# One decoder trunk: the recurrence's square root by a correction step, decay masks as a bound, and the compression with token rows stationary

## The reference, cut to what matters

```python
# NSA: compressed keys and values, 15 blocks of 32 tokens
def compress(t, pe, w):
    ch = t.reshape(B, S // CMP_STRIDE, CMP_STRIDE, d)
    blk = jnp.concatenate([ch[:, :-1], ch[:, 1:]], axis=2)
    return ((blk + pe).reshape(B, nc, CMP_LEN * d) @ w).astype(F32)

# RG-LRU
log_a = -LRU_C * r * jax.nn.softplus(-lam.astype(F32))
a = jnp.exp(log_a)
b = jnp.sqrt(jnp.maximum(-jnp.expm1(2.0 * log_a), 0.0)) * (i_g * xb)
_, h = lax.associative_scan(comb, (a, b), axis=1)      # h_t = a_t h_(t-1) + b_t

# SSD, for each chunk of 128 tokens: Lm is lower triangular
Lm = jnp.exp(segsum(a))
scores = jnp.einsum('bclhn,bcshn->bhcls', Cc, Bc) * Lm
y_diag = jnp.einsum('bhcls,bcshp->bclhp', scores, x)
```

## Time and profile before

| what | us |
|---|---|
| median of 3 runs | 1559.27 (1558.99 to 1560.87) |
| the profiled execution, device time | 1556.36 |
| its span, from first to last instruction | 1554.8 |
| PE busy | 1516.8 (98%) |
| DVE busy | 1249.4 (80%) |
| ACT busy | 1006.7 (65%) |
| loop of the mixers, layer 0 and layer 1 | about 82 to 139 and 481 to 536 |

### The profile page before, as it was taken

One profiled execution on the slowest core, in us unless ns is written; L12 is line 12 of the kernel. 1 busy time (PEld: TensorE's weight loads), 2 busy tenths in 40 slices (PEclk: granted clock), 3 DMA queues, 4 the chain that ended last, 5 costly groups with the idle time before them and its releaser, 6 DMA issues.

```text
span 1554.8 us, 20132 instructions
## 1 busy us (share of the span) xinstructions
PE 1516.8 (98%) x7391; PEld 1272.0 (82%) x7391; DVE 1249.4 (80%) x1296; ACT 1006.7 (65%) x926; POOL 81.5 (5%) x109
## 2 busy tenths in 40 slices
PE   8999999999999899999999999999999999999996
PEld 6987888888798788878888888888888888888885
DVE  6888654455567879998988898899889889889986
ACT  6465534433446647777777777777777777778764
POOL 3101000000000010000000000000000000000000
PEclk9997999999999799999999999999999999999998
DMA  9702655556440049999999999999999999999991
GB/s 316 235 1 59 227 190 189 189 183 195 159 167 1 1 176 341 395 390 353 393 393 348 394 396 347 394 395 346 394 395 344 395 396 343 396 397 346 394 396 59
DMA packets 189820, 444.23 MB, mean 286 GB/s; under 512 B 9697, under 2 KB 15982, under 8 KB 189758
## 3 DMA queue, kind: packets, MB, share of 16 engines
q1 hardware_dynamic: 185206, 427.81, 75.0%
q0 software_dynamic: 4528, 15.58, 3.8%
q10 hardware_dynamic: 24, 0.01, 0.0%
HBM read 435.51 MB, written 7.86 MB: 285 GB/s over the span
## 4 chain that ended last, share of the span: by engine, by line
PE 94%; DVE 3%; ACT 1%; issue 1%; DMA 0%; SPq 0%; POOL 0%; POOLq 0%; DVEq 0%; ACTq 0%
PE bank L439 27%; PE bank L440 27%; PE bank L438 26%; PE bank L569 2%; PE bank L495 2%; PE bank L698 1%; PE bank L572 1%; PE bank L718 1%; PE bank L675 1%; PE bank L727 0%; DVE hT L2051 0%; PE bank L690 0%; PE bank L934 0%; DMA work<-in_nsa_cmp_pe_dram 0%; PE bank L600 0%
## 5 line engine op out<-in xcount | busy, mean ns | idle before, releaser
L1729 DVE TENSOR_TENSOR w_lo<-ring,w_hi 128x2048 fp32r<-128x2048 f32 x372 | 846.5, 2290 | 176.8 <-ACT w_hi L1305 175.8
L1305 ACT ACTIVATE w_hi<-ring 128x2048 fp32r<-128x2048 f32 x372 | 711.8, 1916 | 223.9 <-PE bank L438 223.9
L439 PE MATMUL bank<-w_hi,xT_hi 128*128 128x512 f32 x896 | 353.8, 395 | 0.5 <-DVE xT_lo L2314 0.5
L440 PE MATMUL bank<-w_hi,xT_lo 128*128 128x512 f32 x896 | 349.7, 390 | 0.0
L438 PE MATMUL bank<-w_lo,xT_hi 128*128 128x512 f32 x896 | 240.0, 390 | 0.0
L439 PE MATMUL bank<-w_hi,hidT_hi 128*128 128x512 f32 x560 | 221.0, 395 | 2.8 <-DVE hidT_lo L1736 2.8
L440 PE MATMUL bank<-w_hi,hidT_lo 128*128 128x512 f32 x560 | 218.5, 390 | 0.0
L438 PEld LDWEIGHTS bank<-w_lo,xT_hi 128*128 128x128 f32 x896 | 168.3, 188 | 35.4
L439 PEld LDWEIGHTS bank<-w_hi,xT_hi 128*128 128x128 f32 x896 | 168.3, 188 | 34.5 <-DVE xT_lo L2314 0.7
L440 PEld LDWEIGHTS bank<-w_hi,xT_lo 128*128 128x128 f32 x896 | 168.6, 188 | 33.5
L439 PE MATMUL bank<-w_hi,hT_hi 128*128 128x512 f32 (+2 forms) x384 | 146.8, 385 | 2.7 <-DVE hT_lo L1685 2.7
(11 more groups left out here) (370 smaller groups left out, 1359.0 us busy)
## 6 DMA issues: line engine op xcount, KB each, us to landing
ring<-in_moe_w_gate_dram SPq DMA_DIRECT2D x112, 1024.0 KB, 9.5
ring<-in_moe_w_up_dram SPq DMA_DIRECT2D x112, 1024.0 KB, 9.5
ring<-in_moe_w_down_dram SPq DMA_DIRECT2D x112, 1024.0 KB, 9.2
ring<-in_ffn_w_gate_dram SPq DMA_DIRECT2D x14, 1024.0 KB, 5.1
ring<-in_ffn_w_up_dram SPq DMA_DIRECT2D x14, 1024.0 KB, 5.1
ring<-in_ffn_w_down_dram SPq DMA_DIRECT2D x14, 1024.0 KB, 4.8
ring<-in_w_in_dram SPq DMA_DIRECT2D x12, 1024.0 KB, 6.6
ring<-in_w_out_dram SPq DMA_DIRECT2D x8, 1024.0 KB, 7.2
```

Of the source, the lines that this page charges most:

```text
L439: pe.matmul(o, x_hi, w, start=start, stop=False)
L440: return pe.matmul(o, x_lo, w, start=False, stop=False)
L1305: act.activation(w_hi[:, (base + at) % SPLIT, :], ring[:, i, :], ACT.Copy).then_inc(hi_ready, 1)
L1729: dve.tensor_tensor(w_lo[:, v, :], ring[:, (base + at) % RING, :], w_hi[:, v, :].bitcast(F32), ALU.subtract).then_inc(lo_ready, 1)
```

## The change

- The recurrence. Before, with t = tanh(log_a/2), DVE computed 1/(1 - t) with its reciprocal. Now ACT computes exp(log_a) as well, DVE forms (1 + exp)/2 from it, which is 1/(1 - t) but for rounding, and betters it with one correction step of two instructions. The pieces stand at other steps: the correction and the first `lb` in step 3, the rest of `lb` and `lt2` in step 6, between the first products of `yd` and its sums, with `lt1` and `lgate` ahead of those sums as well.
- The decays. A new constant `dbound` (made by POOL) is 0 where a decay counts and -1e30 where it doesn't. The decay tiles are bounded by it with the minimum that took 0 before, so their exponentials come out as zeros there, and the two mask multiplications go.
- `ssd_sums`, and what DVE does with it, moves from step 3 to step 4, on PE between `scores(4)` and `products(2)`, on DVE behind `score_rows(4)`. Its three fillers go.
- The compression. Before, the weights (128 columns, keys and values together) were stationary and 30 columns of tokens moved, 16 matmuls, with three fillers between. Now the 15 token rows are stationary and 64 columns of weights move, 32 matmuls without fillers. The result lies by rows, so the values need no turning, and the keys do (`turn_keys`). DVE copies it ahead of the convolution of step 2, no longer behind it.
- At the start of layer 0 DVE makes the low part of the first weights between the second and the third group of `hT_lo`, no longer after all four and after the copies of the parameters.

```diff
@@ mixer buffers, constants (POOL)
+        dbound = sb("dbound", [P, 2 * P])
...
+            link(pool.memset(dbound[:, :], 0.0))
...
+            link(pool.affine_select(out=dbound[:, 0:P], in_=dbound[:, 0:P], compare_op=ALU.is_ge, fill=NEG, base=0,
+                                    pattern=[[1, P]], channel_multiplier=-1))
@@ PE
-                def compress(b, idle):
+                def compress(b):
 
                     pe.wait_ge(cin_ready, l + 1)
-                    for j in range(CLEN // 2):
-                        mm = pe.matmul(b[:, 0:2 * NC], w_cmp[:, j, :], cin[:, j, :, :].rearrange("p c n -> p (c n)"),
-                                       start=(j == 0), stop=(j == CLEN // 2 - 1))
-                        if j in (3, 7, 11):
-                            keep_busy(idle, 1)
+                    for c in range(2):
+                        for j in range(CLEN // 2):
+                            mm = pe.matmul(b[0:NC, c * HD:(c + 1) * HD], cin[:, j, c, :], w_cmp[:, j, c * HD:(c + 1) * HD],
+                                           start=(j == 0), stop=(j == CLEN // 2 - 1))
                     give(mm, 0)
 
-                def turn_values():
+                def turn_keys():
 
                     pe.wait_ge(cmp_ready, 2 * l + 1)
                     b = bank(0)
-                    give(pe.transpose(b[0:NC, 0:HD], kcv[HD:P, 1, :], ident[HD:P, HD:P]), 0)
+                    give(pe.transpose(b[0:HD, 0:NC], ckv[0:NC, 0:HD], ident[0:NC, 0:NC]), 0)
...
                 def ssd_sums():
 
                     b = bank(0)
-                    keep_busy(b, 3)
                     pe.wait_ge(ssd_act, 3 * l + 2)
...
                     if n < len(AJ):
                         scores(n)
+                    if n == 4:
+                        ssd_sums()
                     if n >= 2:
                         products(n - 2)
...
                     if n == 3:
-                        turn_values()
-                        ssd_sums()
+                        turn_keys()
@@ ACT, step 1
-                        act.activation(lt2[:, :, :], la[:, :, :], ACT.Tanh, scale=0.5).then_inc(lru_act, 1)
+                        act.activation(lt2[:, :, :], la[:, :, :], ACT.Tanh, scale=0.5)
+                        act.activation(ld[:, :, :], la[:, :, :], ACT.Exp).then_inc(lru_act, 1)
@@ DVE, start of layer 0
-                split_turned(2 * l)
+                if l > 0:
+                    split_turned(2 * l)
                 if l == 0:
+                    split_turned(0, (0, 1))
+                    split(p)
+                    split_turned(0, (2, 3))
...
-                    split(p)
                 split(p + 1)
@@ DVE, the loop
+                    if n == 4:
...
+                        take_bank(dve.tensor_copy(xtok[:, :, :], b[:, :].rearrange("p (t c) -> p t c", t=TB)))
...
+                                link(dve.scalar_tensor_tensor(out=dec0[:, h, :], in0=b[:, i * S:(i + 1) * S],
+                                                              scalar=nacs[:, 0, h:h + 1], in1=dbound[:, :],
+                                                              op0=ALU.add, op1=ALU.min))
+                                ins = dve.scalar_tensor_tensor(out=dec1[:, h, :], in0=b[:, i * S + P:(i + 1) * S],
+                                                               scalar=nacs[:, 1, h:h + 1], in1=dbound[:, 0:P],
+                                                               op0=ALU.add, op1=ALU.min)
...
                     if n == 2:
+                        b = filled()
+                        take_bank(dve.tensor_copy(ckv[0:NC, :], b[0:NC, 0:2 * HD]))
+                        signal(dve.tensor_copy(flag[:, 0:1], ones[:, 0:1]), "cmp", cmp_ready)
                         signal(conv(xbc, xraw, "scw", "scb", 6, 4, 6), "ssd_conv", ssd_conv)
-                        b = filled()
-                        take_bank(dve.tensor_copy(kcv[:, :, :], b[:, 0:2 * NC].rearrange("p (c n) -> p c n", c=2)))
-                        signal(dve.tensor_copy(flag[:, 0:1], ones[:, 0:1]), "cmp", cmp_ready)
...
-                    if n == 4:
+                    if n == 3:
 
                         dve.wait_ge(lru_act, 5 * l + 2)
-                        link(dve.tensor_scalar(ld[:, :, :], lt2[:, :, :], -1.0, 1.0, ALU.mult, ALU.add))
-                        link(dve.reciprocal(ld[:, :, :], ld[:, :, :]))
-                    if n == 5:
+                        link(dve.tensor_scalar(ld[:, :, :], ld[:, :, :], 0.5, 0.5, ALU.mult, ALU.add))
+                        link(dve.scalar_tensor_tensor(out=lb[:, :, :], in0=lt2[:, :, :], scalar=-1.0, in1=ld[:, :, :],
+                                                      op0=ALU.add, op1=ALU.mult))
+                        link(dve.scalar_tensor_tensor(out=ld[:, :, :], in0=lb[:, :, :], scalar=2.0, in1=ld[:, :, :],
+                                                      op0=ALU.add, op1=ALU.mult))
                         link(dve.scalar_tensor_tensor(out=lb[:, :, :], in0=lt2[:, :, :], scalar=-4.0, in1=ld[:, :, :],
                                                       op0=ALU.mult, op1=ALU.mult))
-                        signal(dve.scalar_tensor_tensor(out=lb[:, :, :], in0=lb[:, :, :], scalar=0.0,
...
                     if n == 5:
 
                         dve.wait_ge(ssd_act, 3 * l + 3)
-                        tri = upper[:, :].unsqueeze(1).broadcast_to([P, SSD_H, P])
-                        link(dve.tensor_tensor(dec0[:, :, 0:P], dec0[:, :, 0:P], tri, ALU.mult))
-                        link(dve.tensor_tensor(dec1[:, :, :], dec1[:, :, :], tri, ALU.mult))
...
                     if n == 6:
...
+                        signal(dve.scalar_tensor_tensor(out=lb[:, :, :], in0=lb[:, :, :], scalar=0.0,
+                                                        in1=ld[:, :, :], op0=ALU.max, op1=ALU.mult),
+                               "lru_vec", lru_vec)
+                        link(dve.scalar_tensor_tensor(out=lt2[:, :, :], in0=lt2[:, :, :], scalar=1.0, in1=ld[:, :, :],
+                                                      op0=ALU.add, op1=ALU.mult))
```

More of the change, by code:

```diff
@@ L529, in _ @@
                 p = BASE_MIX[l]
[L530 removed]
+                (qtok, kcat, vtok, xb, xbc, qT, kT, nqT, kswT, kcT, ckv, nacs, cin, xtok, xdt, dec1, kvT2,
                  dec0) = mix_bufs[l]
@@ L1674, in lam_start, with split_turned @@
                        "half_b", half_b_ready)
-            def split_turned(norm):
+            def split_turned(norm, groups=range(4)):
                 l, which = divmod(norm, 2)
                 c0 = PR["ffn" if which else "mix"]
-                for g in range(4):
+                for g in groups:
                     b = filled()
@@ L2021, in _ @@
                         b = filled()
[L2022 removed]
+                        take_bank(dve.tensor_copy(kcT[0:HD, :], b[0:HD, 0:NC]))
                         signal(dve.tensor_copy(flag[:, 0:1], ones[:, 0:1]), "cmp", cmp_ready)
[L2025 to L2030 removed]
@@ L2092, in _ @@
                                                       op0=ALU.add, op1=ALU.mult))
+                        for tb in range(TB):
+                            b = filled()
+                            take_bank(dve.tensor_tensor(yd[:, tb, :], yd[:, tb, :], b[:, 0:GW], ALU.add))
+                        signal(dve.tensor_tensor(yd[:, :, :], yd[:, :, :], zs[:, :, :], ALU.mult), "ssd_vec", ssd_vec)
                     if n == 7:
```

64 lines of the change are left out of this document (24 added, 40 removed).

## The result

| | before | changed |
|---|---|---|
| median | 1559.51 (1558.99 to 1560.87, 4 runs) | 1545.53 (1542.24 to 1546.42, 4 runs) |
| the profiled execution | 1556.36 | 1542.24 |
| ratio | | 0.991, 95% interval 0.9897 to 0.9922 |

The forecast was 1554.4, 4.9 us less, with 1547.5 as the lower end of its range.

A forecast was written before the change was run, and what follows sets the result against it. DVE was taken to bound both mixer loops: -10.7 there, +6.0 for the low clock, -0.2 at the start, -4.9 in all. From 1556.36 that gives 1551.5 profiled; the median, 2.9 above, 1554.4; range 1547.5 to 1562.

The forecast's parts named there:

- The stretches that bound the kernel: Both mixer loops, from DVE's copy of the compressed values to the end of lgate: 34.05 and 32.52 us, DVE the chain.
- DVE's work: Per layer in the stretch: reciprocal out -3.38, correction in +1.44, masks out -1.45, decays reading a second tensor +0.2.
- The two waits for `ssd_sums`: DVE's waits in each layer vanish, as PE runs the sums during DVE's four instructions and score_rows(4): -1.73.
- The new wait of 0.3: DVE at score_rows(4), ready at 102.7, waits for ACT's turned_probs(2), ending at 103.0: +0.3 per layer.
- The compression: Ahead of DVE's copy in step 2: 64 records at 0.06 us, done at 92.15, no loss.
- Rival 2: Compression bound by its 64 records at 0.118 each: DVE waits 3.25 us per layer in step 2, 1560.9; chance 0.18.
- The clock behind PE's gap: PE idles 2 us inside ssd_sums and the clock falls to 1.2 GHz behind it: +6.0 in all; forecast's chance 0.52.
- What the low clock costs: 6.8 us at half speed cost PE 3.4, less 0.4 to spare: DVE waits 3.0 us in each layer.
- The layer 0 wait of 1.53 in step 7: DVE's wait for PE at the low clock; taken to vanish if PE is at the high clock there.
- The tail: After lgate, to the output projection: same chain in both versions, clock taken as low as before, length unchanged within 1 us.
- The start: First low weight part ready before PE wants it: gain 0.2, the middle of 0 to 0.46.
- Rival 1: The clock doesn't fall behind PE's gap, or the gap is covered, so no 6.0 loss: 1548.4; chance 0.12.

The follow-up runs named there:

- e2: Changed kernel with the 3.38 us reciprocal back in place of the correction step, still in step 3: 1550.81 us.
- e9: e8 with the two mask multiplications put back ahead of the products of the decays: 1544.23 us.
- e3: Changed kernel with ssd_sums and DVE's part of it back in step 3, ahead of the correction, without its three fillers: 1554.45 us.
- e6: e3 with the correction moved to step 4, so sums in step 3 and correction in step 4: 1547.56 us.
- e5: Changed kernel with the two mask multiplications put back ahead of the products of the decays: 1543.50 us.
- e7: Kernel before with the move alone: ssd_sums in step 4 without its three fillers, reciprocal in step 3: 1556.51 us.
- e8: Changed kernel with ten filler matmuls per layer in PE's waits of steps 6 to 8: 1541.39 us.
- e16: Changed kernel with the correction alone moved to step 4, so sums and correction both in step 4: 1554.13 us.
- e14: e7 with the ten tail fillers of e8: 1558.80 us.
- e4: Changed kernel with three more DVE instructions of 128x512 per layer ahead of score_rows(4), to lengthen PE's gap: 1549.58 us.
- e10: e8 with e4's three extra DVE instructions per layer ahead of score_rows(4): 1547.22 us.
- e13: Kernel before with the ten tail fillers of e8 and three more ahead of products(3): 1566.48 us.
- e1: The changed kernel again, nothing edited: 1546.03 us.
- The four corners: Sums and correction each in step 3 or 4 of the changed kernel: e1 1546.0, e3 1554.5, e6 1547.6, e16 1554.1 us.

## Why the prediction was wrong

- **The stretches that bound the kernel** were the right ones: 11.2 of the 14 us come from the two mixer loops.
- **DVE's work**: -3.38 + 1.44 - 1.45 + 0.2 = -3.2 forecast per layer, -3.3 measured. The decays with `dbound` took 484 and 351 ns, as before, so 0.2 was too much. e2 gave 4.8 for the reciprocal (3.9 forecast), e9 2.8 for the masks (2.9), part of it a low stretch of the clock.
- **The two waits for `ssd_sums`** went, as forecast, but not for the reason given. With the sums back in step 3 (e3, e6) DVE doesn't wait for them either. So it was not the move that took 1.73 us per layer away, but the three fillers that went or the earlier compression; no run parts the two. The new wait of 0.3 didn't come: DVE left the correction at 102.37 and went on at 102.40, for ACT had turned the probabilities by 102.3.
- **The compression** was right. The row answers rows 6 and 9:

```profile
87.81 3.75 PE L729 MATMUL bank<-w_cmp,work 128*15 128x64 f32 x64
```

  3.67 us to the next row, over 64 records, are 0.057 each, beside the 0.06 taken. DVE's copy stood right behind `score_rows(2)` without a wait. Rival 2 is out. The eight short loads of rows 9 all lay in the low stretch from 124.5 us on, not half of them; at the high clock the new loads show 96 ns.
- **The clock behind PE's gap is the step that failed**, 6.0 of the 8.9 us. The gap was forecast well (2 us, 1.66 measured). The fault was to take the fall of rows 6 and 8 for one that any gap of at least 1.38 us brings. In the changed kernel the clock stayed at 2.4 GHz behind the gap in both layers of both profiles. The traces side by side; a fall counts if it comes within the wait or at most 1.4 us behind its end:

| PE's wait | length, us | loops | the clock |
|---|---|---|---|
| inside `ssd_sums` (changed twice, e5, e7, e8, e9, e16, layer 1 of e14) | 1.60 to 1.85 | 15 | falls in 1 (e14) |
| the same place (e2, e4, e10) | 3.53 to 3.84 | 6 | falls in 5 |
| ahead of `products(3)` (before twice, e6) | 1.38 to 1.69 | 6 | falls in 6 |
| the same place (e3) | 4.32 | 2 | falls in 2 |

  Behind a wait of 1.38 us the clock fell at one place in every loop, behind 1.60 to 1.85 us at the other in one loop of 15; e7 and e14 have the same wait of 1.85, and what parts them is open. Ahead of the first PE had run products of 64 columns, turns and scores with 64 rows; ahead of the second, among others, the sums with 128 rows and columns. What of this decides was not tried. Nor does the wait alone explain the falls: three fillers in it took the fall at `products(3)` away (e13), but the clock also fell with no idle row at all (the changed kernel at 121 us). The Trainium skill ("TensorE: Matmul & The Clock Gate", Why this matters for your kernels) warns only of longer gaps than these; it fits 14 of the 15 loops of the first line and 5 of the 6 of the second, and not the third. I had let one pattern of the trace outvote that rule with 0.52 against 0.12, and the pattern came from another place.
- **What the low clock costs** was too high as well: 1.0 per layer in e10 where I had 3.0. The way to 3.0 counted every microsecond at half speed behind the gap against 0.4 to spare; in e10 DVE waited only 0.9 us for the bank of `ssd_cb` and 0.3 for the products. Most of the error is the length: by the same way 3.4 us at the low level would have cost 3.4/2 - 0.4 = 1.3.
- **The layer 0 wait of 1.53 in step 7** went in the first profile and came back in e1's, 2.0 for the products of step 7 with the clock down since 117 us. It belongs to the spread and not to the change.
- **The tail** behind `lgate` was taken unchanged; it was 12.57 us and is 12.52 in layer 0, and in layer 1 it went from 12.05 to 11.35, a gain of 0.7 that the forecast did not have.
- **The start**: 0.2 forecast, 0.49 in the first profile, but the first scores start at 81.5 to 84.3 us over all traces. What differs is how long the first products, from 12 us on, run slowly (rows of 0.63 us, later 0.40): until 15 us before, until 18 in e1. Neither gain is shown.
- **What is left.** Rival 1, no fall, had 1548.4; measured is 2.9 less. 0.6 is the wait that didn't come, 0.4 the decays. Between the first profiles of the two kernels 0.7 more is the tail of layer 1, and 1.3 lies behind both loops, where the traces differ by up to 3.6 anyway. For the rest: the profiled executions differ by less than the medians, 1556.25 against 1544.65 as means of two, 11.6, where the medians say 13.1 and 14.0. I carried over that the median lies 2.9 above the profiled execution; in the changed kernel it lies 0.9 above the mean of two. Why the kernel before has this offset is open, and with it about 2 us.
- **The move of `ssd_sums`** was reasoned in the wrong unit. I counted waits gone and a wait come for it. The four corners show no price of its own that could be told from the spread.

## What to carry to other kernels

Where three engines hand one chain of steps around, ask how much other work the engine in the lead has between two of its turns. Here it paid to have as much in every interval as covers the way over the others, and not to place each piece where it was ready first. One fall of the clock in a trace is no threshold; look for gaps of the same length behind which it stayed, and price the fall only at the place where it happened. Before small terms are measured, hold the clock still with fillers in waits that are known to be there, and read the loops beside the whole time; the fillers cost the kernel before, whose waits lie elsewhere, 7 us.

## What the hardware showed that I had not expected

- The granted clock fell with PE at work: in both layers of the changed kernel no row of PE shows an idle of its own from 114.22 to the fall at about 121 us (506.07 to 513.4 in layer 1), in products of 64 columns, turns and scores of 15. In e14 it fell at 90.6 us with PE at work in the compression and its fillers.
- The same instructions took 57.99 and 60.78 us; the fall lay at 121 and 117 us, and 17.1 and 23.9 us were at the low level. Ten dense matmuls in PE's waits took the fall away; the mean loop went from 57.8 to 55.1.
- A record with 15 columns of weights and 64 moving columns takes 0.057 us, where those with 128 of weights and 64 moving took 0.118, both at 2.4 GHz.
- A DVE instruction with a column scalar that reads PSUM and a second tensor costs what one without the second tensor does: 484 ns for 256 columns, 351 for 128.
